# Bank copies and evictions ahead of the weight splits in a decoder layer in fp32: ACT and DVE re-ordered, one chunk in other banks, one block's plain units together

## The reference

```python
merged = jax.nn.sigmoid(ga) * (o_a @ w_br_fox[l]) + jax.nn.sigmoid(gb) * (o_b @ w_br_dil[l])
x = x + merged @ w_out[l]
h = rms_norm(x, g_ffn[l])
u = h @ w_up[l]
up = jnp.pad(u, ((0, 0), (CONV_WIDTH - 1, 0), (0, 0)))
wc = w_conv[l]
conv = sum(wc[t] * up[:, t:t + s] for t in range(CONV_WIDTH)) + b_conv[l]
gate, val = jnp.split(conv, 2, axis=-1)
x = x + (jax.nn.silu(gate) * val) @ w_down[l]
```

## Time and profile before

| | us |
|---|---|
| median of 3 runs | 1453.96 (1453.81 to 1454.37) |
| the profiled execution | 1449.69 |
| its span, first to last instruction | 1447.7 |
| TensorE busy in it | 1395.0 (96%) |
| DVE busy | 968.3 (67%) |
| ACT busy | 771.8 (53%) |
| DMA engines, mean rate | 199 GB/s of HBM read and written |

### The profile page before, as it was taken

The page is one execution under the profiler, slowest core; times in us unless marked ns, Lnnn a source line. Parts: engine busy times, 40 slices in busy tenths (PEclk is TensorE's granted clock), DMA queues, the critical chain, the costliest instruction groups (busy, mean ns, idle before and its releaser), DMA issues.

```text
span 1447.7 us, 16263 instructions
## 1 busy us (share of the span) xinstructions
PE 1395.0 (96%) x6285; PEld 1145.1 (79%) x6285; DVE 968.3 (67%) x1196; ACT 771.8 (53%) x962; POOL 103.5 (7%) x123
## 2 busy tenths in 40 slices
PE   9999999999999999999789999999999999999999
PEld 7888888888888888878568777878787878777777
DVE  5646465654555466566586878777787878687876
ACT  6555454554555444456465655565565555565552
POOL 0112120100000000000010000001010101000000
PEclk9999999999999999999899999999999999999999
DMA  9755555556666555777486868686878777777753
GB/s 326 253 167 159 165 163 166 167 169 191 186 187 188 190 181 187 247 215 215 150 198 193 233 188 241 169 258 175 255 170 269 178 257 189 234 207 220 214 168 109
DMA packets 111021, 289.53 MB, mean 200 GB/s; under 512 B 11232, under 2 KB 11488, under 8 KB 110432
## 3 DMA queue, kind: packets, MB, share of 16 engines
q1 hardware_dynamic: 98528, 250.83, 53.1%
q0 software_dynamic: 9504, 34.61, 13.5%
q10 hardware_dynamic: 2912, 3.06, 0.6%
HBM read 286.36 MB, written 2.10 MB: 199 GB/s over the span
## 4 chain that ended last, share of the span: by engine, by line
PE 81%; DVE 9%; ACT 4%; DMA 4%; issue 2%; SPq 0%; ACTq 0%
PE acc L390 18%; PE acc L392 18%; PE acc L391 18%; PE acc L408 5%; DVE w_lo L1052 4%; PE acc L412 4%; PE acc L410 4%; DMA raw<-w_down 3%; PE acc L423 3%; PE acc L427 3%; PE acc L425 3%; ACT w_hi L750 2%; DVE work L1310 2%; PE acc L615 1%; ACT work L957 1%
## 5 line engine op out<-in xcount | busy, mean ns | idle before, releaser
L1052 DVE TENSOR_TENSOR w_lo<-raw,w_hi 128x1024 fp32r<-128x1024 f32 x399 | 484.9, 1223 | 353.9 <-ACT w_hi L750 350.6
L750 ACT ACTIVATE w_hi<-raw 128x1024 fp32r<-128x1024 f32 x399 | 419.7, 1059 | 462.2 <-PE acc L392 306.4
L390 PE MATMUL acc<-w_hi,actA 128*128 128x512 f32 x1116 | 444.6, 398 | 13.7 <-DVE actA L1323 8.9
L392 PE MATMUL acc<-w_hi,actA 128*128 128x512 f32 x1116 | 435.2, 390 | 0.0
L391 PE MATMUL acc<-w_lo,actA 128*128 128x512 f32 x1116 | 434.7, 390 | 0.0
L390 PEld LDWEIGHTS acc<-w_hi,actA 128*128 128x128 f32 x1116 | 209.6, 188 | 63.5 <-DVE actA L1323 13.1
L392 PEld LDWEIGHTS acc<-w_hi,actA 128*128 128x128 f32 x1116 | 209.5, 188 | 44.6
L391 PEld LDWEIGHTS acc<-w_lo,actA 128*128 128x128 f32 x1116 | 209.8, 188 | 41.4
L408 PE MATMUL acc<-w_hi,actB 128*128 128x512 f32 x352 | 139.2, 396 | 19.4 <-ACT odd L1032 18.4
L750 ACT ACTIVATE w_hi<-raw_y 128x1024 fp32r<-128x1024 f32 x88 | 93.2, 1061 | 95.5 <-DVE raw_y L1056 34.1
L1052 DVE TENSOR_TENSOR w_lo<-raw_y,w_hi 128x1024 fp32r<-128x1024 f32 x88 | 107.3, 1221 | 51.8 <-ACT w_hi L750 51.8
(11 more groups left out here) (171 smaller groups left out, 1354.2 us busy)
## 6 DMA issues: line engine op xcount, KB each, us to landing
raw<-w_in SPq DMA_DIRECT2D x159, 512.0 KB, 3.7
raw<-w_up SPq DMA_DIRECT2D x88, 512.0 KB, 4.4
raw<-w_down SPq DMA_DIRECT2D x88, 512.0 KB, 4.5
raw_x<-w_up SPq DMA_DIRECT2D x44, 512.0 KB, 5.4
raw_y<-w_up POOLq DMA_DIRECT2D x44, 512.0 KB, 6.1
raw<-w_out SPq DMA_DIRECT2D x32, 512.0 KB, 4.2
raw_y<-w_up SPq DMA_DIRECT2D x22, 512.0 KB, 4.2
raw_x<-w_up POOLq DMA_DIRECT2D x22, 512.0 KB, 5.5
```

The source lines that it names most:

```text
L390: nc.tensor.matmul(o, lhsT=a_h, rhs=w_hi[:, s, k, :], start=first and k == 0, stop=False)
L392: mm = nc.tensor.matmul(o, lhsT=a_l, rhs=w_hi[:, s, k, :], start=False, stop=last and k == KU - 1)
L750: nc.scalar.activation(w_hi[:, n % RING, :, :], src.rearrange("p (k n) -> p k n", k=KU), ACT.Copy).then_inc(hi_done, 1)
L1052: nc.vector.tensor_tensor(w_lo[:, n % RING, :, :], src.rearrange("p (k n) -> p k n", k=KU), w_hi[:, n % RING, :, :].bitcast(f32), ALU.subt ...
```

## The change

1. At each slot, ACT does the copy out of bank 0 (`running_sum`) ahead of the split, and DVE does `add_down`, the results and chunk 3's `add_x2` (`empty_banks`) ahead of it. Before, they stood behind the split of their slot. The result c22 moves from the slot of P2's first unit to that of D0, ahead of its split.
2. The high part of the hidden activation moves one slot forward on ACT, its low part one slot forward on DVE.
3. Chunk 2 of the out-projection goes into banks 6 and 7. So P3 of block 0, which writes bank 1, waits for the add of chunk 1 alone, and O's first unit waits for that of chunk 2.
4. In block 0 all four gate U stand together, ahead of P2. The copies and parts of chunk 3 are moved to fit: ACT's `x2t_copy(3)` and `plain_high(3)` come one slot sooner, DVE's `plain_low(3)` and the low part for P4 stand at the first gate U. The gate copy waits for the low parts of six products in place of seven. The scaling of block 0's val sums moves to the slots of the first two val U.

```diff
@@ -62,7 +62,7 @@
-            units += plain(1, 0, 1) + product("P2") + plain(1, 2, 3) + product("P4") + plain(0, 0, 1, 2, 3)
+            units += plain(1, 0, 1, 2, 3) + product("P2") + product("P4") + plain(0, 0, 1, 2, 3)
@@ -588,15 +588,13 @@
             for c in range(3):
-                R, banks = OUT0 + c, bank[2 * (c % 2):2 * (c % 2) + 2]
+                R, banks = OUT0 + c, bank[(0, 2, 6)[c]:(0, 2, 6)[c] + 2]
...
                 elif c == 1:
                     pe.wait_ge(merged, 4)
-                else:
-                    pe.wait_ge(x2_done, c - 1)
@@ -637,7 +635,7 @@
                     elif name == "P3":
-                        pe.wait_ge(x2_done, 3)
+                        pe.wait_ge(x2_done, 2)
@@ -701,6 +699,8 @@
                 if unit[0] == "O":
                     u = unit[2]
+                    if u == 0:
+                        pe.wait_ge(x2_done, 3)
@@ -972,7 +972,37 @@
+            def running_sum(n, unit):
+
+                i = unit[1]
+                if unit == ("S", i, "P1", QU - 1):
+                    act.wait_ge(used, n + 1)
...
+                    nc.scalar.activation(val[0], bank[0][:, :], ACT.Copy, scale=nrs2[:, 0:1] if i else -1.0)\
+                        .then_inc(p1_copied, 1)
+                elif unit == ("S", i, "P6", QU - 1):
...
+                    nc.scalar.activation(val[1], bank[0][:, :], ACT.Copy, scale=nrs2[:, 1:2] if i else -1.0)\
+                        .then_inc(v_copied, 1)
+                elif unit == ("S", i, "P5", QU - 1):
...
+                        act.wait_ge(part_lo, len(STEPS) - 1)
+                    nc.scalar.activation(gate[0], bank[0][:, :], ACT.Copy, scale=xrs2[:, 0:1] if i else 1.0)\
+                        .then_inc(u0_copied, 1)
+                elif unit == ("U", i, 1, PLAIN - 1):
...
+                    nc.scalar.activation(gate[1], bank[0][:, :], ACT.Copy, scale=xrs2[:, 1:2] if i else 1.0)\
+                        .then_inc(u1_copied, 1)
+
             for n, unit in enumerate(FFN, FF_UNIT):
+                if unit == ("S", 1, "P1", QU - 1):
+                    newest_tap(0, 1)
+                running_sum(n, unit)
                 high(n + RING)
@@ -999,38 +1029,15 @@
-                    elif side == 1 and j == 1 and i:
+                    elif side == 1 and j == 0 and i:
                         hidden_high(i - 1)
-                    elif side == 1 and j == 0 and i == 0:
-                        x2t_copy(3, bank[4:6])
-                        plain_high(3)
...
+                elif name == "P5" and q == 1 and i == 0:
+                    x2t_copy(3, bank[4:6])
+                    plain_high(3)
@@ -1344,6 +1351,8 @@
             def scaled(i, r, part, order):
                 if i == 0:
+                    if order > 2:
+                        dve.wait_ge(v_copied, 1)
@@ -1351,12 +1360,36 @@
+            def empty_banks(n, unit):
+
+                kind, i = unit[0], unit[1]
+                if kind == "D" and unit[2] % 2 == 1:
+                    add_down(n, i, unit[2] // 2)
+                elif unit == ("D", i, 0) and i < BLOCKS - 1:
+                    dve.wait_ge(u1_copied, i + 2)
+                    result(bank[3][:, :], nrs2[:, 1:2], gate[1], c22_done)
+                elif unit == ("U", i, 1, PLAIN - 1):
+                    dve.wait_ge(used, n + 1)
+                    dve.wait_ge(u0_copied, i + 1)
+                    scaled(i, 0, gate[0], 1)
+                    result(bank[1][:, :], xrs2[:, 0:1], gate[0], c12_done)
+                    if i == 0:
+                        dve.wait_ge(u1_copied, 1)
+                        scaled(0, 1, gate[1], 2)
+                        result(bank[3][:, :], nrs2[:, 1:2], gate[1], c22_done)
+                elif unit == ("U", i, 0, PLAIN - 1):
+                    dve.wait_ge(used, n + 1)
+                    dve.wait_ge(v_copied, i + 1)
+                    result(bank[2][:, :], xrs2[:, 0:1], val[0], c11_done)
+                    result(bank[3][:, :], xrs2[:, 1:2], val[1], c21_done)
+                elif unit == ("O", 3, UPR - 1):
+                    add_x2(n, 3, bank[6:8])
+
             for n, unit in enumerate(FFN, FF_UNIT):
+                empty_banks(n, unit)
                 low(n + RING)
@@ -1372,46 +1405,25 @@
-                    elif side == 1 and j == 2 and i:
+                    if side == 1 and j == 1 and i:
                         hidden_low(i - 1)
                     elif side == 1 and j == 0 and i == 0:
+                        plain_low(3)
+                        part_low("P4")
+                    elif side == 1 and j == 1 and i == 0:
                         dve.wait_ge(rs_x, 2)
                         nc.vector.tensor_scalar(nrs2, xrs2, -1.0, None, ALU.mult).then_inc(nrs_ready, 1)
...
                     elif side == 0 and j < 2:
                         older_tap(i, 0, 1 - j)
+                        if i == 0:
+                            scaled(0, j, val[j], 3 + j)
```

More of the change, by code:

```diff
@@ L1001, in _ @@
                         gate_silu(i)
-                    elif side == 1 and j == PLAIN - 1:
-                        act.wait_ge(used, n + 1)
-                        nc.scalar.activation(gate[1], bank[0][:, :], ACT.Copy, scale=xrs2[:, 1:2] if i else 1.0)\
-                            .then_inc(u1_copied, 1)
-                    elif side == 1 and j == 1 and i:
+                    elif side == 1 and j == 0 and i:
                         hidden_high(i - 1)
-                    elif side == 1 and j == 0 and i == 0:
-                        x2t_copy(3, bank[4:6])
-                        plain_high(3)
                     continue
                 _, i, name, q = unit
-                if name == "P1" and q == 0 and i:
+                if name == "P1" and q == 0 and i > 1:
                     newest_tap(i - 1, 1)
-                elif name == "P1" and q == QU - 1:
-                    act.wait_ge(used, n + 1)
-                    if i:
-                        act.wait_ge(val_ready, i)
-                        act.wait_ge(nrs_ready, 1)
-                    nc.scalar.activation(val[0], bank[0][:, :], ACT.Copy, scale=nrs2[:, 0:1] if i else -1.0)\
-                        .then_inc(p1_copied, 1)
-                elif name == "P6" and q == QU - 1:
-                    act.wait_ge(used, n + 1)
-                    nc.scalar.activation(val[1], bank[0][:, :], ACT.Copy, scale=nrs2[:, 1:2] if i else -1.0)\
-                        .then_inc(v_copied, 1)
-                elif name == "P5" and q == QU - 1:
-                    act.wait_ge(used, n + 1)
-                    if i:
-                        act.wait_ge(gate_ready, i)
-                    else:
-                        act.wait_ge(part_lo, len(STEPS))
-                    nc.scalar.activation(gate[0], bank[0][:, :], ACT.Copy, scale=xrs2[:, 0:1] if i else 1.0)\
-                        .then_inc(u0_copied, 1)
+                elif name == "P5" and q == 1 and i == 0:
+                    x2t_copy(3, bank[4:6])
+                    plain_high(3)
                 elif name == "P4" and q == 1:
@@ L1289, in _ @@
                     dve.wait_ge(x_again, 16)
-                add_x2(UPR * R + UPR - 1, c, bank[2 * (c % 2):2 * (c % 2) + 2])
+                add_x2(UPR * R + UPR - 1, c, bank[(0, 2, 6)[c]:(0, 2, 6)[c] + 2])
             def x2_norm():
@@ L1357, in _ @@
                     _, i, u = unit
-                    if u % 2 == 1:
-                        add_down(n, i, u // 2)
                     if i == BLOCKS - 2 and u == LATE - 1:
@@ L1374, in _ @@
                         part_low("P2")
-                    elif u == 7:
-                        add_x2(n, 3, bank[6:8])
                     continue
```

37 lines of the change are left out of this document (11 added, 26 removed).

## The result

The changed kernel takes **1409.3 us** (median of 4 runs, 1409.1 to 1410.8) against 1453.9 us before (4 runs beside them, 1452.5 to 1454.4): ratio 0.9697, 95% interval 0.968 to 0.9714. Forecast was 1405.0, with a range of 1396 to 1419. Measured again later on another chip it is 1408.9 against 1453.9, ratio 0.9693 (0.9671 to 0.9715).

What follows compares the result with a forecast made beforehand. TensorE, busy nearly always, was taken as the bound, losing time to single ACT or DVE instructions. Gains of 12.9 + 11.6 + 5.8 + 1.4 + 17.1 = 48.8 us off 1453.96 gave 1405 us, range 1396 to 1419.

Steps and rivals of the forecast that it cites:

- gate copy, blocks 2 to 10: First plain unit's wait for the gate copy: one split fewer ahead of it, gain 12.9 us, about 5 left.
- hidden low part before D0: First down unit's wait for the hidden activation's low part, blocks 1 to 10: all gone, gain 11.6 us.
- add before D6: TensorE's wait before D6 for the down-projection's add: gone with the add before the split, gain 5.8 us.
- last val results: Wait at the end for the last block's val results, now before D1's split: gain 1.4 us.
- first blocks: Stalls and lost clock in blocks 0 and 1: 27.6 us before, 10.5 left, gain 17.1, between 12 and 20.
- The rival with the transfers: Transfers set the gate copy's pace; none of the 0.7 us comes back, 1412 to 1416 us; chance 0.17.
- 1.0 + 0.5 + 2.5 + 1.8 + 1.7: Waits left in blocks 0 and 1: third chunk's first unit, first gate copy, third plain unit, P6, P5; 7.5 us.
- I take the same gain for all: The 48.8 us gain, worked on the profiled 1449.69 us run, was also taken off the 1453.96 us median.
- Slower: Rival: splits come late once DVE's split of D7 slips beyond its 1.8 us margin; 1465 us, chance 0.02.
- under 6 us in sum: Sign in the trace after: the gate copy's waits total under 6 us.
- two waits of about 2 us in block 1: Sign in the trace after: TensorE waits at P6, some 1.8 us, and at P5, 1.7 us.
- still stands over 2 us behind: Sign of being wrong: the gate copy is still over 2 us behind.

Runs made afterwards that it cites:

- the split behind the copy: Changed kernel, but from block 1 on ScalarE does the gate copy before the splits of the two P5 slots: 1397.97 us.
- five buffers: Changed kernel with the last stage's down, plain and out-projection tiles rotating over five buffers instead of four, so transfers are issued one tile earlier: 1395.24 us.
- the first three undone together: Changed kernel with copies and evictions back behind the splits and the hidden tile's splits one slot later, all at once: 1444.91 us.
- the version without a gap over 1.2 us in blocks 0 and 1: Changed kernel extended with all copies first, plus block 1's second running-sum copy ahead of the first plain tile's split: 1389.84 us.

## Why the prediction was right, and where it was not

The mechanism held, part by part: the kernel waits where one instruction stands behind others in an in-order queue, and such stalls add up. Its sum, held against the two profiled executions (gain in us, lost time of a stall in full):

| term | predicted | measured |
|---|---|---|
| gate copy, blocks 2 to 10 | 12.9 | 8.4 |
| hidden low part before D0 | 11.6 | 11.8 |
| add before D6 | 5.8 | 6.0 |
| last val results | 1.4 | 1.4 |
| first blocks | 17.1 | 12.7 |
| sum | 48.8 | 40.3 (spans: 40.4) |

**The step that was mis-sized** is the gate copy: 5 us left were predicted, 9.9 are. The working had 1.4 us a block for the split that no longer stands between, 0.7 for an earlier load and -0.65 for a TensorE that comes sooner, 1.45 in all. The idle time of these nine blocks went from 15.5 to 7.4 us, 0.9 a block. What is missing is most of the 0.7: against the start of the first plain unit, ACT took the fourth tile 0.2 us later on average before and takes it 0.6 us later now (from both traces, blocks 2 to 10), where the working had it unmoved. The landing didn't keep up with TensorE. Two things make that up. SP requests the tile 4.36 us ahead of that unit, where it was 4.50, so the request moved forward by some 0.5 and not by 0.7. In block 3 before it was this row, with the unit at 889.26:

```profile
884.77 0.33 SPq L312 DMA_DIRECT2D raw<-w_up  x1
```

And the transfer takes longer: from request to landing 4.98 us on average (4.90 in the second measurement), where it took 4.66. The rival with the transfers had this second cause; it left 12 us, and the truth lies between. That the copy's stall is the split's wait for this tile is shown by the experiments with the split behind the copy and with five buffers. Why the transfer takes 0.2 to 0.3 longer wasn't tried; the DMA engines are busy for 0.78 of block 3 and not for 0.76.

**In the first blocks** the step that failed is the list of what is left, "1.0 + 0.5 + 2.5 + 1.8 + 1.7": it has no place for block 1's gate copy. The 0.49 of before was taken as gone, and 2.07 stands there, since block 1 has no D7 and the copy's neighbour in the queue is D0's tile, asked for only at 735.61. P6 in block 1 is 0.5 longer than worked out, and the last turn still waits 0.49. With what came out shorter set against them, these are 3.1 us of the 4.4; the rest is on the other side of the sum, where the kernel before lost some 1 us less than the 27.6 of the working. Of the clock one fall was forecast, and there is one, but in the first profile it stands behind block 1's gate copy and only in the second behind the third plain unit.

**The error in the sum was partly paid back by the base.** The sum was made on an execution of 1449.69 us and then taken off the median of 1453.96. That execution is shorter than all 32 others of the kernel before that were taken with or after the result (1450.3 to 1463.5). From the profiled execution the same sum gives 1400.9, and the changed kernel's was 1409.15. So the step "I take the same gain for all" hid 4.3 of 8.3 us, and that the forecast came as near as 4.3 is luck to that extent.

**One rival was summed wrongly.** In "Slower", the 4.9 us that a block gains are the 48.8 over ten blocks, which hold the gain of the first blocks already; "less the head's gain of 17" counts it again. Nothing in the forecast rests on it.

**What was right**: no wait for the hidden part, for the add or before P4; the gate copy right behind one raw split; about 1 us before O's first unit; 2 to 3 before the third plain unit; a block of 64.5 to 65.5 us (65.46). Of the signs listed, "under 6 us in sum" failed (9.8). The place of the fall of the clock failed in one of two profiles. Of "two waits of about 2 us in block 1" there are three, and the third is the gate copy's: with 2.07 us it meets "still stands over 2 us behind" there, while in blocks 2 to 10 its longest is 1.4 (1.7 in the second profile).

Undone one at a time, the parts cost 10.2, 15.0, 11.8, 1.2 and 3.7 us, 41.9 in sum by medians and 31 by ratios, of the 45.0 between the two kernels. With the first three undone together, 9.0 us to the kernel before are left on the same chip, more than the 4.9 that the banks and the unit order cost when undone alone. The clock is a part of that: the profile of the kernel before has four falls from the out-projection on, that of the three parts undone has one.

## What to carry to other kernels

In front of an in-order engine's instruction that the bottleneck waits for, look for one that waits itself, for a transfer above all. Either move it behind, or issue its transfer one buffer sooner: both took the same ten stalls away. When such a queue is re-ordered, re-read the first passes of the loop by themselves, since their neighbours differ. And make a sum against several executions of the kernel before, or at least ask where the profiled one lies among them.

## What the runs showed of the hardware

**The same gap doesn't always bring the clock down.** The third plain unit of block 0, in the second measurement of the changed kernel, and the six microseconds from there in it:

```profile
696.34 0.50 PE L408 MATMUL acc<-w_hi,actB 128*128 128x512 f32 x1 [2.47 <-DVE actB L1131]
...
696.00:702.00 6.00, 5.66 (x18) 4.50 (x19) 2.11 (x4) 0.96 (x1) 0.00 (x0) 0.72 0.54 175
```

In the first measurement, after 2.48 us of idle time at the same unit:

```profile
696.00:702.00 6.00, 5.95 (x26) 4.91 (x27) 3.17 (x5) 1.19 (x2) 0.00 (x0) 1.00 0.49 169
```

A stretch at the lower level (1.2 of 2.4 GHz) costs 1.2 to 3.0 us in these traces, mostly 1.6. In the thirteen profiles, from the out-projection on, the eight gaps of TensorE of more than 2.5 us were all followed by one, and of 37 gaps between about 1.8 and 2.5 us eleven were. The Trainium skill ("TensorE: Matmul & The Clock Gate", "HAM oscillation — how this bites in real kernels") says that idle gaps between bursts of matmuls throw the clock to its lower level; the traces agree, and show besides that the length of the one gap doesn't tell. What else decides wasn't tried. It is a part of the spread of kernels with such gaps: the version without a gap over 1.2 us in blocks 0 and 1 ran at a mean clock of 1.000 four times, within 0.8 us.
